# A two-layer encoder trunk on one core: rows times gamma moved to VectorE, the first high part on VectorE, an earlier copy of the sums, and down blocks 32 to 55 in twelve places

## The chip, the cores and the metric

The kernel runs on one core of a Trainium2 chip. The metric is the device time of one execution in microseconds, lower is better. Engines: TensorE (PE) multiplies, VectorE (DVE), ScalarE (ACT) and GpSimd (POOL) work elementwise, SyncE (SP) only issues DMAs. DMAs are issued here by three engines' queues: SP's (q1 in the profile), ACT's (q10) and POOL's gathers (q0).

## The reference

Two layers over 256 tokens of width 1024. The first mixes tokens by dilated attention and pooling, the second by a gated unit; each is followed by a product-key retrieval (`peer`), in which every token takes 128 of 16384 experts:

```python
q = (ht @ w_q).reshape(T, PEER_HEADS, 2, PEER_HALF_DIM)          # ht = rms_norm(x) * gamma
scores = jnp.einsum('thic,hikc->thik', q, sub_keys)
sv, si = lax.top_k(scores, PEER_TOPK)                            # 16 of 128 in each half
cand = sv[:, :, 0, :, None] + sv[:, :, 1, None, :]
best, ci = lax.top_k(cand.reshape(T, PEER_HEADS, 256), PEER_TOPK)
gate = jax.nn.softmax(best, axis=-1)
hid = gelu(einsum('cd,ckd->ck', xb, w_down[eb]))
out = einsum('ck,ckd->cd', gb * hid, w_up[eb])
```

A final RMS norm ends the program. All inputs and the output are float32.

## The kernel before

**Mixing and queries.** Products with the mixer's and the query weights are made as three products of split numbers: a weight block of 128 x 1024 lands in `raw` (four places), `high_part` (ACT, L705) rounds it into `w_hi`, and `low_part` (POOL, L614) subtracts the two into `w_lo` (two places). The activations are split in the same way into `hT_hi` (ACT, L720) and `hT_lo` (DVE, L1453). A layer has 40 such blocks, the last 16 of them for the queries. A next `raw` load waits for `w_lo` of the block that it overwrites (`load`, L468), and a next `w_lo` waits until PE is done with the block two before (L613). The last block of each group of eight waits for its low part before its first product (L1262).

**Normed rows.** Between the query blocks DVE (`norm_tokens`, L1421) works out 1/rms, writes two small scale matrices (L1424), and the first 128 tokens' normed rows `hn` (L1428). POOL waits for them ahead of its low part of query block 5 and multiplies them by gamma, in place in `gff` (L640 to L643). PE multiplies the scale matrices ahead of query block 5 (L1241), DVE copies the result (L1431) and makes `hT` from it (L1437), on which the down phase works. ACT, SP and DVE wait for the product in `gff` by the semaphore `hng_done`.

**Down and up.** 160 tokens ("dense") are multiplied by all 16384 experts' down rows, in 128 blocks of 512 KB, eight matmuls each (`down`, L1292), and later by the up rows (128 blocks, loaded in pairs of 1 MB). For the other 96 tokens only the chosen experts' rows are gathered by POOL (L635), one 512 KB indirect DMA for 128 rows: 96 gathers with down rows and 96 with up rows in a layer. Gather q of the first 53 is issued no sooner than PE has done `pace(q)` = q * 71 // 53 down blocks (L625), no more than five are in flight (L621), and there are ten places (`RING`). DVE takes the dot products of the gathered rows (L1605) between the pieces of its search for the best experts (L1584 to L1699). Results of down blocks (`take_hidden`, L877) fill the arena from its start, over what lay there.

**Where the down blocks lie.** Blocks 0 to 31 use sixteen places: four of `raw`, four of `w_raw`, and eight in the arena (`extra`). From block 32 only the first eight places are used. So SP issues block 16 + j when block j is done, for j = 0 to 23 (L548 to L556; ahead of j = 8 it issues two 1 MB pairs of up rows). It then waits for the first softmax gates (`idg_done`, L557) and moves them with four small DMAs (L559). From block 40 on the load of block b is issued when block b - 8 is done. Of these, blocks 40 to 79 alternate: even ones are issued by SP (`load_down_even`, L539), odd ones by ACT (`load_between`, L944, at L949). From block 80 SP issues all.

**The end of a layer.** ACT takes four banks of the up sums (`UP_BANKS`, L1027) in turn; ahead of the third it copies half of the sparse tokens' sums to other partitions (L1024), which DVE adds to `xs` (L1778) before it adds the dense results (L1814). In the last layer the final norm follows (L693, L1407 to L1417, L1820).

Of the kernel before, what the change touches and what calls it, by code (L numbers as in the profile page):

```python
# [11 lines left out]
ALU = mybir.AluOpType  # L12
# [4 lines left out]
LAYERS = 2  # L17
SEQ = 256
TILES = SEQ // P
DM = 1024  # L20
# [24 lines left out]
BLOCKS = KEYS  # L45
# [20 lines left out]
WIDE_TO = 2 * WIDE  # L66
ROWS = PICKS + MORE
# [14 lines left out]
MORE_AT, MORE_TAKE_AT, MORE_GATES_AT = 26, 34, 40  # L82
# [5 lines left out]
ONES_FROM, ROWS_AT, ONES = 30, 8, 432  # L88
# [99 lines left out]
assert EXTRA_AT + EXTRA_SOON * DM <= QT_AT and ONES_FROM + RAW - 2 >= WIDE_TO - 1  # L188
assert all(WIDE + DOWN_RAW + k <= (EXTRA_AT + k * DM) // DENSE for k in range(EXTRA))
RING_AT = BLOCKS * DENSE  # L190
# [23 lines left out]
def build_trunk(nc, x_d, consts_d, gfin_d, tab_d, iota_d, lncount_d, poolm_d, poolw_d,  # L214
                pscale_d, wm_d, ws_d, bs_d, cnorm_d, subk_d, wd_d, wu_d, gff_d, rows_d, up_rows_d, out_d):
    ctx = ExitStack()
    with ctx:
# [207 lines left out]

        narrow_from = WIDE_TO // WIDE
        down_fills, mix_fills = narrow_from + (BLOCKS - WIDE_TO) // DOWN_RAW, MIX_BLOCKS // RAW
# [4 lines left out]

        def down_slot(b):

            j = b % WIDE
            if b < WIDE_TO and j >= DOWN_RAW:
                return extra[j - DOWN_RAW]
            return down_raw[b % DOWN_RAW]

        def down_arrival(b, l):  # L440

            j = b % WIDE
            if b < WIDE_TO and j >= DOWN_RAW:
                return extra_full[j - DOWN_RAW], (l * narrow_from + b // WIDE + 1) * 16
            j, filled = b % DOWN_RAW, b // WIDE if b < WIDE_TO else narrow_from + (b - WIDE_TO) // DOWN_RAW
# [18 lines left out]
        def _(sp):  # L464
            for l in range(LAYERS):
# [63 lines left out]
                sp.wait_ge(hng_done, l + 1)  # L529
# [18 lines left out]
                for j in range(WIDE + DOWN_RAW):  # L548
                    if j == DOWN_RAW:
                        for p in range(UP_EARLY):  # L550
                            load_up(p, p)
                    sp.wait_ge(w_used, l * LAYER + MIX_BLOCKS + j + 1)
                    if DOWN_RAW <= j < WIDE:
                        load_extra(WIDE + j, j - DOWN_RAW)
                    else:
                        load_down(WIDE + j, j % DOWN_RAW)  # L556
# [38 lines left out]
            for t, k in ((0, 0), (1, 0), (1, 1)):  # L595
# [3 lines left out]
                else:  # L599
                    sp.wait_ge(hn_done, TILES * LAYERS + k + 1)  # L600
# [4 lines left out]
        def _(pool):  # L605
            for l in range(LAYERS):
# [1298 lines left out]
```

## Time and profile before

| | us |
|---|---|
| median of 3 runs | 1501.04 (1500.75 to 1506.45) |
| profiled execution, its own time | 1499.63 |
| its span (first to last instruction) | 1497.8 |
| PE busy | 1470.0 (98%) |
| DVE, POOL, ACT busy | 913.3, 735.3, 488.9 |
| mean granted TensorE clock | 0.996 |
| HBM read | 519 MB, 347 GB/s over the span |

The profile is of one execution; its own time lies 1.4 us below the median. Instruction rows give the start, how long, the engine and line, what is written and read, and in brackets the engine's idle time before with what ended it. Times are from the span's start. Rows with a count merge neighbours of one kind.

### The profile page before, as it was taken

How to read it: one execution, taken by the hardware profiler on the slowest of the kernel's cores; microseconds unless marked ns; L12 is line 12 of the kernel's file. 1: busy time of each engine (PE TensorE's matmuls, PEld its weight loads, DVE VectorE, ACT ScalarE, POOL GpSimd, SP SyncE). 2: the span in 40 equal slices, each digit the busy share in tenths (PEclk: the TensorE clock that was granted, in tenths of full speed). 3: DMA queues.
4: the chain of work that ended last, by engine and by line, in shares of the span. 5: the costliest groups of instructions: out<-in, count | busy, mean ns of one | idle time of the engine just before them, and what ended most of it. 6: DMA issues, size and time to landing. Idle time of an engine off the chain costs nothing.

```text
span 1497.8 us, 28995 instructions
## 1 busy us (share of the span) xinstructions
PE 1470.0 (98%) x10604; PEld 1436.4 (96%) x10604; DVE 913.3 (61%) x2981; ACT 488.9 (33%) x1206; POOL 735.3 (49%) x632
## 2 busy tenths in 40 slices
PE   8999999999999999999999999999999999999996
PEld 6889999999999999999988999999999999999996
DVE  1744999748875444354633499995587834444654
ACT  5663323258870000000065532221888400000001
POOL 6577232348885233343467843323688733333540
PEclk9999999999999999999999999999999999999998
DMA  6456999999999999999945679999899999999994
GB/s 224 160 189 216 359 408 407 406 356 341 361 356 412 415 417 416 417 415 417 376 152 199 212 238 408 407 407 399 319 346 361 372 417 416 416 416 417 415 397 182
DMA packets 126273, 522.86 MB, mean 349 GB/s; under 512 B 14800, under 2 KB 15056, under 8 KB 109392
## 3 DMA queue, kind: packets, MB, share of 16 engines
q1 hardware_dynamic: 56752, 240.01, 42.7%
q0 software_dynamic: 55296, 201.35, 33.9%
q10 hardware_dynamic: 14112, 80.04, 13.1%
q8 instruction: 65, 1.06, 0.3%
q14 instruction: 48, 0.39, 0.1%
HBM read 519.22 MB, written 1.05 MB: 347 GB/s over the span
## 4 chain that ended last, share of the span: by engine, by line
PE 85%; DMA 6%; issue 2%; ACT 2%; DVE 2%; POOL 2%; SPq 0%; DVEq 0%; POOLq 0%; ACTq 0%
PE ps L1042 85%; DMA arena<-in_rows,ret 2%; DMA raw<-in_wd 2%; POOL w_lo L614 2%; DMA spare<-in_wu 1%; PE ps L1050 1%; ACT arena L693 0%; SPq L559 0%; ACT w_hi L705 0%; ACT hT_hi L720 0%; DMA xs<-in_x 0%; DVE xs L1814 0%; DMA raw<-in_wm 0%; DVE arena L1605 0%; DVE xs L1778 0%
## 5 line engine op out<-in xcount | busy, mean ns | idle before, releaser
L1042 PE MATMUL ps<-arena,raw 128*128 128x160 f32 (+1 forms) x2688 | 379.2, 300 | 3.0 <-DMA raw<-in_wd 3.0
L1042 PE MATMUL ps<-arena,w_raw 128*128 128x160 f32 (+1 forms) x2688 | 377.4, 299 | 1.1 <-DVE arena L1732 1.1
L635 POOL DMA_INDIRECT arena<-in_up_rows,ret x192 | 206.5, 1076 | 347.3 <-DVE oh_buf L1745 181.7
L1042 PEld LDWEIGHTS ps<-arena,raw 128*128 128x128 f32 x2688 | 369.8, 191 | 3.5 <-DMA raw<-in_wd 3.5
L1042 PEld LDWEIGHTS ps<-arena,w_raw 128*128 128x128 f32 x2688 | 368.2, 190 | 1.5 <-issue 1.5
L635 POOL DMA_INDIRECT arena<-in_rows,ret x192 | 200.9, 1046 | 257.9 <-DMA arena<-in_rows,ret 72.3
L1745 DVE SCALAR_TENSOR_TENSOR oh_buf<-arena,ret,oh_buf 128x1024 f32<-128x1024 f32 x126 | 163.0, 1294 | 171.7 <-DMA arena<-in_up_rows,ret 165.1
L614 POOL TENSOR_TENSOR w_lo<-raw,w_hi 128x1024 fp32r<-128x1024 f32 x80 | 193.9, 2433 | 93.4 <-PE ps L1042 67.3
L1042 PE MATMUL ps<-arena 128*128 128x160 f32 (+5 forms) x1336 | 184.6, 302 | 0.5 <-DMA spare<-in_wu 0.4
L1042 PEld LDWEIGHTS ps<-arena 128*128 128x128 f32 (+2 forms) x1336 | 178.0, 189 | 3.2 <-issue 1.8
L1605 DVE SCALAR_TENSOR_TENSOR arena<-arena,ps 128x1024 f32<-128x1024 f32 x128 | 153.8, 1216 | 4.0 <-DMA arena<-in_rows,ret 4.0
L1745 DVE SCALAR_TENSOR_TENSOR ret<-arena,ret 128x1024 f32<-128x1024 f32 x62 | 79.7, 1285 | 113.5 <-DMA arena<-in_up_rows,ret 109.9
L651 POOL TENSOR_SCALAR oh_buf<-iota,ret 128x128 f32<-128x128 f32 x160 | 126.6, 795 | 26.8 <-issue 12.4
L999 ACT ACTIVATE arena<-ret 32x1024 f32<-32x1024 f32 x6 | 6.3, 1054 | 395.7 <-PE ps L1042 139.1
L877 ACT ACTIVATE arena<-ps 128x160 f32<-128x160 f32 x152 | 46.0, 302 | 243.6 <-PE ps L1042 223.6
L705 ACT ACTIVATE w_hi<-raw 128x1024 fp32r<-128x1024 f32 x80 | 83.5, 1060 | 80.8 <-DMA raw<-in_wm 53.6
L933 ACT ACTIVATE ret<-iota,ret 128x128 f32<-128x128 f32 x320 | 100.8, 386 | 2.6 <-PE ps L1042 2.6
L1671 DVE SCALAR_TENSOR_TENSOR arena<-iota,ret,ps 128x54 f32<-128x54 f32 x512 | 100.3, 269 | 0.0
L1726 DVE TENSOR_TENSOR arena<-arena,ps 128x512 f32<-128x512 f32 x80 | 55.0, 688 | 67.4 <-PE ps L1042 34.5
L1605 DVE SCALAR_TENSOR_TENSOR arena<-arena,spare 128x1024 f32<-128x1024 f32 x64 | 77.5, 1223 | 19.7 <-DMA arena<-in_rows,ret 19.6
L1042 PE MATMUL ps<-oh_buf,ret 128*128 128x128 f32 x640 | 84.4, 275 | 1.1 <-ACT ret L941 1.1
L1042 PE MATMUL ps<-arena,spare 128*128 (+1 forms) x576 | 82.2, 299 | 0.0
(149 smaller groups left out, 1799.8 us busy)
## 6 DMA issues: line engine op xcount, KB each, us to landing
raw<-in_wd SPq DMA_DIRECT2D x92, 512.0 KB
w_raw<-in_wd SPq DMA_DIRECT2D x92, 512.0 KB
raw<-in_wm SPq DMA_DIRECT2D x80, 512.0 KB
low_rows<-in_wu SPq DMA_DIRECT2D x18, 1024.0 KB
arena<-in_wu SPq DMA_DIRECT2D x18, 1024.0 KB
arena<-in_wd SPq DMA_DIRECT2D x32, 512.0 KB, 13.9
raw<-in_wu SPq DMA_DIRECT2D x14, 1024.0 KB
raw<-in_wu ACTq DMA_DIRECT2D x14, 1024.0 KB
```

Source lines behind the costliest of these rows:

```text
L614: nc.gpsimd.tensor_tensor(w_lo[:, s % WLO, :], raw[:, s, :], whs[:, s].bitcast(F32), ALU.subtract).then_inc(wlo_pool, 1)
L635: nc.gpsimd.indirect_dma_start(ring[s], None, table, bass.IndirectOffsetOnAxis(ap=index, axis=0)).then_inc(row_full[s], 16)
L651: nc.gpsimd.tensor_scalar(oh1g[:, g % 2, k, :], iota[:, :], i1T[:, t:t + 1], gT[:, t:t + 1], ALU.is_equal, ALU.mult).then_inc(oh1_pool, 1)
L705: nc.scalar.activation(whs[:, s], raw[:, s, :], ACT.Copy).then_inc(whi_done, 1)
L877: nc.scalar.activation(block_of(b), down_psum(b % SLOTS), ACT.Gelu_apprx_tanh).then_inc(h_done, 1)
L933: nc.scalar.activation(oh2[:, g % 2, k, :], iota[:, :], ACT.Abs, scale=-1.0, bias=i2T[:, t:t + 1]).then_inc(oh2_far, 1)
L1042: return nc.tensor.matmul(out, lhsT, rhs, start=start, stop=stop, skip_group_check=shared)
L1050: last = nc.tensor.transpose(ps[:, bank + banks[i], o:o + P], src[:, t, c * P:(c + 1) * P], ident[:, :])
L1605: nc.vector.scalar_tensor_tensor(row, row, 1.0, more_rows if more else h_rows, ALU.mult, ALU.mult, accum_out=(more_hid if more else row_hi ...
L1671: step(nc.vector.scalar_tensor_tensor(found[:, (j * 8 + k) % 24, :], places, cif[:, t, n:n + 1], pay[:, h, :], ALU.is_equal, ALU.mult, acc ...
L1726: nc.vector.tensor_tensor(part, part, gates, ALU.mult).then_inc(gmul_done, 1)
L1745: ins = nc.vector.scalar_tensor_tensor(out, row, coef[:, j:j + 1], out, ALU.mult, ALU.add)
```

## The change

Four things are done.

1. DVE multiplies xs by 1/rms and by gamma in one instruction a half, straight into `gff`; POOL's product and `hn` go.
2. The high part of block 0 of layer 0 is made by DVE, as its second instruction, and ACT waits for it in place of making it.
3. In the last layer the copy of the sums stands ahead of bank 1 and not of bank 2.
4. Down blocks 32 to 55 use twelve places (the eight and the last four of the arena's). SP issues all of blocks 16 to 55; the gates' four DMAs come behind block 55's; even and odd blocks alternate between SP and ACT only from 56 on. `write_ones`, which fills the part of the arena behind those places, comes 24 blocks later.

```diff
+MIDDLE, MIDDLE_EXTRA = DOWN_RAW + EXTRA // 2, EXTRA // 2
+MIDDLE_TO = WIDE_TO + 2 * MIDDLE
-MORE_AT, MORE_TAKE_AT, MORE_GATES_AT = 26, 34, 40
+MORE_AT, MORE_TAKE_AT, MORE_GATES_AT = 26, 34, MIDDLE_TO
-ONES_FROM, ROWS_AT, ONES = 30, 8, 432
+ONES_FROM, ROWS_AT, ONES = 54, 8, 432
...
+        def down_place(b):
+
+            if b < WIDE_TO:
+                return b % WIDE, b // WIDE
+            if b < MIDDLE_TO:
+                j, filled = (b - WIDE_TO) % MIDDLE, WIDE_TO // WIDE + (b - WIDE_TO) // MIDDLE
+                return j if j < DOWN_RAW else j + EXTRA - MIDDLE_EXTRA, filled
+            return b % DOWN_RAW, narrow_from + (b - MIDDLE_TO) // DOWN_RAW
...
-                for j in range(WIDE + DOWN_RAW):
-                    if j == DOWN_RAW:
+                for b in range(WIDE, MIDDLE_TO):
+                    if b == WIDE + DOWN_RAW:
                         for p in range(UP_EARLY):
                             load_up(p, p)
-                    sp.wait_ge(w_used, l * LAYER + MIX_BLOCKS + j + 1)
-                    if DOWN_RAW <= j < WIDE:
-                        load_extra(WIDE + j, j - DOWN_RAW)
+                    j, filled = down_place(b)
+                    last = max(n for n in range(b) if down_place(n)[0] == j)
+                    sp.wait_ge(w_used, l * LAYER + MIX_BLOCKS + last + 1)
+                    if j >= DOWN_RAW:
+                        load_extra(b, j - DOWN_RAW)
                     else:
-                        load_down(WIDE + j, j % DOWN_RAW)
+                        load_down(b, j)
                 sp.wait_ge(idg_done, TILES * l + 1)
...
                 for b in range(MIX_BLOCKS):
-                    if b == Q_FROM + 5:
-                        pool.wait_ge(gff_loaded, 16 * (l + 1))
-                        pool.wait_ge(hn_done, TILES * (l + 1))
-                        nc.gpsimd.tensor_tensor(gff, gff, hn[:, 0, :], ALU.mult).then_inc(hng_done, 1)
                     low_part(b, b % RAW, first=l == 0 and b < WLO)
...
                         if l == 0 and first == 0:
-                            high_part(0, 0, first=True)
+                            act.wait_ge(whi_done, 1)
...
                 for g, chunks in enumerate(UP_BANKS):
-                    if g == 2:
+                    if g == (2 if l + 1 < LAYERS else 1):
                         act.wait_ge(row_used, (l + 1) * GATHERS)
...
+                dve.wait_ge(gff_loaded, 16 * (l + 1))
                 for k in range(2):
                     ks = slice(k * HALF, (k + 1) * HALF)
-                    nc.vector.tensor_scalar(hn[:, 0, ks], xs[:, 0, ks], rinv[:, 2, 0:1], None,
-                                            ALU.mult).then_inc(hn_done, 1)
+                    nc.vector.scalar_tensor_tensor(gff[:, ks], xs[:, 0, ks], rinv[:, 2, 0:1], gff[:, ks], ALU.mult,
+                                                   ALU.mult).then_inc(hng_done, 1)
...
             nc.vector.memset(primed[:, :], 0.0).then_inc(primed_set, 1)
+            dve.wait_ge(raw_full[0], 16)
+            nc.vector.tensor_copy(whs[:, 0], raw[:, 0, :]).then_inc(whi_done, 1)
             dve.wait_ge(consts_loaded, 16)
```

The waits for `hng_done` count to 2 * (l + 1) now, and `down_slot` and `down_arrival` take place and fill from `down_place`.

## Rows read from the trace of the kernel before

**Rows 1.** PE's waits, the longest of layer work: us in total, times, longest.
```profile
PE ps L1042 <- DMA raw<-in_wd: 3.0, 2, 2.7
PE ps L1042 <- POOL w_lo L614: 2.5, 6, 0.7
```
**Rows 2.** Timeline, start of the kernel, ACT and PE.
```profile
7.62 1.05 ACT L705 ACTIVATE w_hi<-raw 128x1024 fp32r<-128x1024 f32 x1
8.81 2.04 PE L1042 MATMUL ps<-w_hi,hT_hi 128*128 128x512 f32 x4 [1.18 <-ACT w_hi L705]
...
19.81 1.08 PE L1042 MATMUL ps<-w_lo,hT_hi 128*128 128x512 f32 x4
```
**Rows 3.** Timeline of layer 1's query phase, DVE and POOL.
```profile
836.87 2.41 DVE L1413 SCALAR_TENSOR_TENSOR rtmp<-rinv 128x2 f32<-128x2 f32 x1
842.34 0.87 DVE L1428 TENSOR_SCALAR arena<-xs,rinv 128x512 f32<-128x512 f32 x2
...
843.35 2.39 POOL L643 TENSOR_TENSOR arena<-arena 128x1024 f32<-128x1024 f32 x1 [1.22 <-DVE arena L1428]
845.70 9.46 POOL L614 TENSOR_TENSOR w_lo<-raw,w_hi 128x1024 fp32r<-128x1024 f32 x4
```
**Rows 4.** The same stretch on PE.
```profile
848.16 1.22 PE L1042 MATMUL ps<-hT_hi,w_lo 128*128 128x256 f32 x8 [0.24 <-POOL w_lo L614]
...
851.13 1.12 PE L1042 MATMUL ps<-hT_hi,w_lo 128*128 128x256 f32 x8
852.96 0.36 PE L1042 MATMUL ps<-hT_hi,w_hi 128*128 128x256 f32 x1 [0.70 <-POOL w_lo L614]
```
**Rows 5.** Timeline of the down phases on PE, four blocks a row.
```profile
234.07 8.86 PE L1042 MATMUL ps<-arena,w_raw 128*128 128x160 f32 x64
243.23 7.06 PE L1042 MATMUL ps<-arena,raw 128*128 128x160 f32 x50 [0.31 <-DMA raw<-in_wd]
...
975.99 7.24 PE L1042 MATMUL ps<-arena,raw 128*128 128x160 f32 x39 [2.70 <-DMA raw<-in_wd]
```
**Rows 6.** Windows: PE, PEld, DVE, ACT, POOL busy (x), PEclk, DMA share, GB/s.
```profile
179.00:228.00 49.00, 49.00 (x363) 49.00 (x362) 46.83 (x270) 10.81 (x33) 15.85 (x17) 1.00 1.03 410
976.00:980.00 4.00, 4.00 (x19) 4.00 (x20) 4.00 (x23) 0.41 (x2) 0.00 (x0) 0.64 1.04 410
```
**Rows 7.** DMA queues from 929 to 958: packets, MB, share of 16 engines.
```profile
q0 software_dynamic: 1622, 5.92, 51.3%
q1 hardware_dynamic: 1617, 5.89, 50.9%
```
**Rows 8.** The same from 970 to 1007.9, two of the three queues.
```profile
q1 hardware_dynamic: 1361, 4.91, 32.6%
q10 hardware_dynamic: 1157, 4.20, 27.9%
```
**Rows 9.** All DMA and the gathers' queue, 155.7 to 277.4, layer 0.
```profile
DMA packets 13074, 47.97 MB, mean 394 GB/s; under 512 B 1652, under 2 KB 1652, under 8 KB 12805
...
q0 software_dynamic: 5375, 19.59, 40.5%
```
**Rows 10.** The same from 886.2 to 1007.9, layer 1.
```profile
DMA packets 12977, 47.62 MB, mean 391 GB/s; under 512 B 1642, under 2 KB 1642, under 8 KB 12705
...
q0 software_dynamic: 5455, 19.88, 41.2%
```
**Rows 11.** Gathers with down rows issued from 155 to 277.4 (layer 0).
```profile
L635 POOL DMA_INDIRECT arena<-in_rows,ret x39: 932/932/1796, 164.1 to 274.7; - x39
```
**Rows 12.** DMA issues from 175 to 209: KB each, median us to landing.
```profile
arena<-in_wd SPq DMA_DIRECT2D x8, 512.0 KB, 22.9
```
**Rows 13.** Timeline of SP's queue in layer 1: the gates, then blocks 40 and 42.
```profile
941.90 5.68 SPq L559 DMA_DIRECT2D stats<-ret  x4
958.26 4.68 SPq L514 DMA_DIRECT2D raw<-in_wd  x2
```
**Rows 14.** Timeline of the kernel's end, DVE.
```profile
1486.31 1.28 DVE L1814 TENSOR_TENSOR xs<-xs,ps 128x512 f32<-128x512 f32 x2 [0.56 <-PE ps L1372]
```

More of the change, by code:

```diff
@@ L187 @@
 EXTRA_AT, EXTRA_SOON = 4608, 4
-assert EXTRA_AT + EXTRA_SOON * DM <= QT_AT and ONES_FROM + RAW - 2 >= WIDE_TO - 1
+assert EXTRA_AT + EXTRA_SOON * DM <= QT_AT and ONES_FROM + RAW - 2 >= MIDDLE_TO - 1
 assert all(WIDE + DOWN_RAW + k <= (EXTRA_AT + k * DM) // DENSE for k in range(EXTRA))
+assert all(MIDDLE_TO - EXTRA + k <= (EXTRA_AT + k * DM) // DENSE for k in range(MIDDLE_EXTRA, EXTRA))
+assert MIDDLE_TO % DOWN_RAW == 0
 RING_AT = BLOCKS * DENSE
@@ L424, in blocks @@
                     body(i * slots + j, j)
-        narrow_from = WIDE_TO // WIDE
-        down_fills, mix_fills = narrow_from + (BLOCKS - WIDE_TO) // DOWN_RAW, MIX_BLOCKS // RAW
+        narrow_from = WIDE_TO // WIDE + (MIDDLE_TO - WIDE_TO) // MIDDLE
+        down_fills, mix_fills = narrow_from + (BLOCKS - MIDDLE_TO) // DOWN_RAW, MIX_BLOCKS // RAW
         fills = mix_fills + down_fills
         down_raw = [raw[:, s, :] for s in range(RAW)] + [w_raw[:, s, :] for s in range(WHI)]
+        def down_place(b):
[5 more added lines that the diff above has]
+            return b % DOWN_RAW, narrow_from + (b - MIDDLE_TO) // DOWN_RAW
         def down_slot(b):
[L435 to L438, printed above, removed]
+            j, _ = down_place(b)
+            return extra[j - DOWN_RAW] if j >= DOWN_RAW else down_raw[j]
         def down_arrival(b, l):
[L442 to L445, printed above, removed]
+            j, filled = down_place(b)
+            if j >= DOWN_RAW:
+                per_layer = narrow_from if j - DOWN_RAW >= MIDDLE_EXTRA else WIDE_TO // WIDE
+                return extra_full[j - DOWN_RAW], (l * per_layer + filled + 1) * 16
             if j < RAW:
@@ L527, in _ @@
                     load_extra(DOWN_RAW + k, k)
-                sp.wait_ge(hng_done, l + 1)
+                sp.wait_ge(hng_done, 2 * (l + 1))
                 sp.wait_ge(w_used, l * LAYER + MIX_BLOCKS)
@@ L546, in load_up @@
                                  ).then_inc(up_full[p], 16)
-                for j in range(WIDE + DOWN_RAW):
-                    if j == DOWN_RAW:
+                for b in range(WIDE, MIDDLE_TO):
+                    if b == WIDE + DOWN_RAW:
                         for p in range(UP_EARLY):
                             load_up(p, p)
-                    sp.wait_ge(w_used, l * LAYER + MIX_BLOCKS + j + 1)
-                    if DOWN_RAW <= j < WIDE:
-                        load_extra(WIDE + j, j - DOWN_RAW)
+                    j, filled = down_place(b)
+                    last = max(n for n in range(b) if down_place(n)[0] == j)
+                    sp.wait_ge(w_used, l * LAYER + MIX_BLOCKS + last + 1)
+                    if j >= DOWN_RAW:
+                        load_extra(b, j - DOWN_RAW)
                     else:
-                        load_down(WIDE + j, j % DOWN_RAW)
+                        load_down(b, j)
                 sp.wait_ge(idg_done, TILES * l + 1)
@@ L599, in _ @@
                 else:
-                    sp.wait_ge(hn_done, TILES * LAYERS + k + 1)
+                    sp.wait_ge(hn_done, k + 1)
                 sp.dma_start(out_d[:, t, ks], hn[:, t, ks]).then_inc(out_stored, 16)
@@ L918, in take_rows @@
                 def take_rows():
-                    act.wait_ge(hng_done, l + 1)
+                    act.wait_ge(hng_done, 2 * (l + 1))
                     act.wait_ge(pair_found, PIECES * l + PIECES // 2)
@@ L1433, in norm_tokens @@
                 settle()
-                dve.wait_ge(hng_done, l + 1)
+                dve.wait_ge(hng_done, 2 * (l + 1))
                 for c in range(DC):
@@ L1631, in search @@
                         dve.wait_ge(sc_sb, 8 * (l + 1))
-                        dve.wait_ge(hng_done, l + 1)
+                        dve.wait_ge(hng_done, 2 * (l + 1))
                         step(nc.vector.tensor_copy(numbers, iota[:, :]))
```

## Prediction

> **What bounds the kernel now.** I read the page first, then PE's waits, the timeline around each wait, and last the DMA queues in windows. The page has PE at 98% of the span, so nearly all of the 1497.8 us is matmuls that the change doesn't touch; what can be won is the time in which PE waits or runs at the low clock. The waits name two causes inside the layers: down blocks that land late, 3.0 us in two waits, and POOL's low parts, 2.5 us in six [rows 1]. A third stands at the start, where PE waits 1.18 us for ACT's first high part [rows 2]. So all four edits together have some 8 us within reach, and the one that shifts DMA traffic can lose more than that.
>
> **First high part on DVE.** ACT makes `w_hi` from 7.62 in 1.05 us, between two pairs of `hT_hi`, and PE starts at 8.81 [rows 2]. ACT's row shows no wait for data, so the block had landed by 7.62. DVE is idle then. Its copy of 128x1024 isn't in the trace; the nearest row is its scaling of two halves of 128x512 in 0.87 us [rows 3], the other side is ACT's 1.05. PE also needs the first `hT_hi`, done about 0.1 us after 7.62, so it can start up to 0.95 us sooner, and at worst no sooner. POOL's first low part moves with it. What it is worth depends on the clock: the first four matmuls took 2.04 us and four later ones 1.08 [rows 2], the levels 1.2 and 2.4 GHz. If the clock rises at the same moment as before, 0.9 us at the low level is worth 0.4; if it rises with the work, 0.9. I take **-0.4**, between 0 and -0.95.
>
> **Rows times gamma.** In the query phase POOL multiplies by gamma at 843.35, for 2.39 us, ahead of low part 5, and then makes four low parts back to back from 845.70 [rows 3]. PE catches up twice: eight matmuls from 851.13 take 0.96 us at 0.12 each, and the next starts at 852.96, 0.87 late, of which the row calls 0.70 idle; by the same measure the wait of 0.24 at 848.16 is 0.41 [rows 4]. That is 1.28 us a layer. Without the product low part 5 can start once PE has left block 3. PE wants low part 5 at 847.75; back from there 16 matmuls, some 0.6 us of scale products and one block of 24 matmuls (2.9 us) give 842.3, with the handover 842.6, against 845.70. What is added is DVE's: two halves with two operands in SBUF, for which the nearest is an add of two 128x512 halves in 1.28 us [rows 14], in place of 0.87 [rows 3]. Here lies a hazard that the trace shows: DVE's L1413, 128x2 with two operands in SBUF, took 2.41 us while POOL made a low part, and L1428 only ran behind one [rows 3]. So either POOL waits up to 1.28 us, and ends low part 5 at 846.3 at the latest, 1.4 us ahead of PE's need, or DVE waits up to 2.4 and delays `hT`, which PE wants only at block 8, at 855.8. Low part 7 is wanted at 852.1 and would be ready near 851.1. The waits for `hng_done` on ACT and SP have far more slack: both act in the down phase. I take the whole, 2 x 1.28 = **-2.5**; if the cover of 1.0 us is gone by a further blocked low part (2.4), it is +1.4 a layer, so between -2.6 and +2.8.
>
> **The copy of the sums.** Of the last four dense adds the second pair waits 0.56 us for PE's own last transposes [rows 14], and the rest of the end follows from it. An earlier copy lets only the first pair start earlier. **0**, between -0.3 and 0.
>
> **Twelve places.** One block is 0.524 MB, 1.28 us at the 410 GB/s that all queues move together [rows 6]. PE takes a block every 2.17 us (49 us for 363 records, 16 a block [rows 6]). While only SP and the gathers have work, they send equal numbers of packets [rows 7], so SP lands a block every 2.56 us, slower than PE eats. Loads were landing 22.9 us after their issue, ten blocks later [rows 12]: SP's queue is backed up, and a block in it lands no sooner for having been given a place sooner. What ends that state in the kernel before is ACT's queue, which takes every second block from 41 on: then the two move 9.11 MB in 37.9 us [rows 8], a block in 2.18 us, just PE's pace. The change puts all of blocks 40 to 55 back on SP's queue and lets ACT join 16 blocks later. Against that stand four more places, and the gates' DMAs (5.68 us of issuing at 941.90, then block 40 at 958.26 [rows 13]) no longer ahead of block 40 but ahead of block 56. Block 56 is still issued only when block 48 is done.
>
> I make a budget up to the moment when PE would begin block 56 with no stall. Block 40 began at 243.23 and 975.99, 0.47 and 2.87 us late (the rows ahead of them end a block grid of 2.17; the page calls 0.31 and 2.70 of it idle [rows 5]), so block 56 is due at 277.4 and 1007.9. By 277.4 all queues moved 47.97 MB, 19.59 of it gathers [rows 9]; less 0.16 MB of code fetches that is 53.8 blocks' worth for the down queues and 37.4 gathers. After the change the total is the same, but with two queues gathers get half, until their pace stops them: at block 56 it allows 41.8, against 39 issued before [rows 11], and two are in flight, so 39.7 will have landed, 2.3 more. That leaves 51.5. The down side wants the rest of block 7 (0.5), blocks 12 to 15 (4), the rows for the 32 tokens (1), two up pairs (4) and blocks 16 to 56 (41), 50.5; and ACT's queue will by then have taken blocks 57, 59 and half of 61 out of order, 2.5 more. It is short by 1.5. In layer 1 the moved total is 47.62 MB, 19.88 of it gathers [rows 10]: 52.6 and 37.9, after the change 50.8, short by 2.2. A missing block costs 1.28 us if the gathers give way when PE, and with it their pace, stops, and 3.84 if three queues share evenly: 1.9 to 5.8 us in layer 0, 2.8 to 8.4 in layer 1. I take 3.0 and 4.5, nearer to the low ends. Against the old stalls that is (3.0 - 0.47) + (4.5 - 2.87) = +4.2. The old one in layer 1 also brought the low clock: from 976 to 980 PE was granted 0.64 and did 19 records where 30 fit (363 in 49 us), 1.5 us [rows 6]. That stays, and layer 0's new stall of about the old one's length gets it with even odds, +0.7. Together **+4.9**, between -4.8 (no stall and no low clock at all) and +13.
>
> The ones that ACT writes come 24 blocks later, ahead of the phase that reads them, on an engine busy 10.81 of 49 us [rows 6]: nothing.
>
> A rule of the Trainium skill speaks against this sum: DMA: Bandwidth & Descriptors, Rules for kernel authors, says that spreading DMAs over the issuing engines for bandwidth doesn't help and saves issue time only. By it SP alone would bring what SP and ACT brought, and the sum for this edit would be -4.8. The trace here disagrees: the second queue got 1157 packets of its own beside 1361 [rows 8], and the two together took 60.5% of the engines' time where SP alone had 50.9% [rows 7]. The same page's section Queues, rings and completion order, that each DMA engine goes round its queues packet by packet, fits rows 7 and 8.
>
> **Sum.** -0.4 - 2.5 + 0 + 4.9 = +2.0 us against the profiled execution's 1499.63; the median lies 1.4 above it, so 1501.04 + 2.0 = **1503**. 0.5%, about 7.5 us, is what a measurement can tell from no change.
>
> **Rivals.**
> - *The stall is gone.* SP keeps up through block 55, for instance because the gathers stay behind their pace or the backlog has drained by then; the four places give 8.7 us of lead. For it: the longest wait stands at block 40, right at the change from sixteen places to eight. Against it: the equal shares of rows 7. -0.4 - 2.5 - 4.8 = -7.7, **1493.3**. Chance 0.26.
> - *The stall moves to block 56 at its old size.* The budget is short, but by less than I have it. -0.4 - 2.5 = -2.9, **1498**. Chance 0.17.
> - *The low parts are blocked in turn.* DVE's two halves and POOL's low parts lock each other out so that nothing is won there: 1503 + 2.5 = **1505.5**. For it: the 2.41 us of rows 3; against: the 1.0 us of cover. Chance 0.08.
> - *Slower: SP's queue starves at its join with ACT's.* From ACT's first load at block 49 SP has a third, blocks 50 to 56 come every 3.8 us, and PE stops in pieces, with the low clock in both layers: the upper ends, 5.8 and 8.4 us, give +10.9, with two low clocks +12.4, less 2.9, +9.5, **1510.5**. It decides from 7.5 us more than before, that is 10.4 us of added stalls. For it: 22.9 us from issue to landing, and the backlog only grows until block 49. Against it: the gathers stop at their pace. Chance 0.14.
>
> The forecast has the remaining 0.35. Faster by over 0.5% is the first rival, 0.26; slower by over 0.5% the last, 0.14; within it the rest, 0.60. The range is 1492 to 1509.5: it takes in the first rival with all of the start's gain and most of the last.
>
> **What would show it.** Right: PE's waits for `raw<-in_wd` gone at block 40 and back at or just before block 56 in both layers, near 277 and 1005, longer in layer 1; SP and gathers with equal packets up to about 265 and 995; the low clock behind the stalls. POOL's six waits down to four or fewer, low parts in the query phase never back to back for more than two. PE's first product at 7.9 to 8.6. The last four adds unmoved against PE's last transposes. Wrong: no wait for down blocks in either layer, or a total wait above 10 us; SP's queue landing blocks 40 to 55 at 2.2 us each or faster; a wait for `hT` at query block 8.

## The result and the profile after

The changed kernel took 1513.55 us, the median of six runs (1510.56 to 1514.69), where the kernel before took 1500.89 beside it (six runs, 1498.09 to 1506.45). The ratio is 1.0083, with a 95% interval of 1.0063 to 1.0103. It is slower by some 12.6 us; 1503.0 was forecast, in a range that ended at 1509.5. The profiled execution took 1510.56 us, with a span of 1508.8; it is the fastest of the six, so what follows is the changed kernel at its best. One execution of a kernel below (e3, 1689.88 us at a mean granted clock of 0.85) was in a slow state and is left out of every number.

PE's waits in the changed kernel (us in total, times, longest), where before had [rows 1]:

```profile
PE ps L1051 <- DMA raw<-in_wd: 6.8, 3, 3.4
...
PE ps L1051 <- DMA arena<-in_wd: 6.0, 6, 1.5
PE ps L1051 <- DMA w_raw<-in_wd: 2.2, 2, 1.1
...
PE ps L1051 <- POOL w_lo L627: 0.3, 1, 0.3
```

Down blocks account for 15.0 us in eleven waits instead of 3.0 in two; the low parts went from 2.5 us in six waits to 0.3 in one. So VectorE's part did its work and the blocks' loads lost much more than it won. PE's timeline in layer 0 shows where; block 40 starts at 240.05, block 44 at 249.11, block 56 at 286.70 (compare [rows 5]):

```profile
240.05 8.86 PE L1051 MATMUL ps<-arena 128*128 128x160 f32 x64
249.11 10.12 PE L1051 MATMUL ps<-arena,raw 128*128 128x160 f32 x64 [0.21 <-DMA raw<-in_wd]
259.36 5.00 PE L1051 MATMUL ps<-arena,w_raw 128*128 128x160 f32 x32
265.43 4.98 PE L1051 MATMUL ps<-arena,w_raw 128*128 128x160 f32 x32 [1.07 <-DMA w_raw<-in_wd]
271.66 2.44 PE L1051 MATMUL ps<-arena 128*128 128x160 f32 x16 [1.25 <-DMA arena<-in_wd]
274.40 2.44 PE L1051 MATMUL ps<-arena 128*128 128x160 f32 x16 [0.29 <-DMA arena<-in_wd]
278.31 5.01 PE L1051 MATMUL ps<-arena 128*128 128x160 f32 x32 [1.47 <-DMA arena<-in_wd]
286.70 3.53 PE L1051 MATMUL ps<-arena,raw 128*128 128x160 f32 x24 [3.38 <-DMA raw<-in_wd]
```

Block 40's wait is gone. From block 44 on each block starts 2.56 instead of 2.17 us after the one before: the row from 249.11 holds four blocks in 10.12 us where the row above it holds four in 8.86, although PE is hardly called idle in it, since it waits between the records of one row. From block 50 on the pieces are larger. Against blocks that follow one another in 2.17 us from block 0 on, block 56 starts 11.9 us late in layer 0 and 11.0 in layer 1. In the kernel before it was 0.6 and 4.7 us late: the stalls of 0.47 and 2.87 at block 40, and the low clock behind the second. (The 15.0 us of the page are less than 11.9 + 11.0, since it leaves out most of the small waits.) No low clock follows here: outside the start and the last 8 us the granted clock is 1.00. In the five other executions the mean granted clock was 0.993 to 0.995 against 0.997 here, which for this span is an estimated 6 to 13 us more at the low level; so some of them most likely had it, and that would be the 3 us that the median lies above this profile. No trace of them was kept.

The same by stages, from PE's first matmul of one stage to that of the next, in us. "Down phase" in the table and in the experiments is the stretch from the first down matmul to the first matmul of the gates, which stands behind block 76 (77 blocks of the 128):

| stage | before | after | difference |
|---|---|---|---|
| first to second transposes of `xs` (start) | 11.39 | 9.35 | -2.04 |
| query phase, layer 0 and 1 | 57.25, 57.27 | 55.89, 55.89 | -1.36, -1.38 |
| down phase, layer 0 | 169.66 | 179.77 | +10.11 |
| down phase, layer 1 | 172.43 | 178.93 | +6.50 |
| last gate matmul to up phase, layer 0 and 1 | 27.31, 26.63 | 26.51, 26.50 | -0.80, -0.13 |
| last matmul to the end of the span | 11.8 | 11.88 | +0.1 |

Of the 169.66 us before, 1.37 come from a wait for ScalarE (`ret`, L941; 1.1 by the page) just ahead of the gates and not for a block. `xs` also landed 0.7 us later in this execution. Together, with differences of at most 0.4 us in the stages not shown, that is the spans' 11.0 us.

DMA queues of the changed kernel while SP's loads and the gathers are alone, from 205 to 262 (packets, MB, share of 16 engines), to be set beside [rows 7]:

```profile
q1 hardware_dynamic: 3195, 11.61, 51.2%
q0 software_dynamic: 3191, 11.61, 51.0%
```

They are again in step: 11.61 MB in 57 us is a block (0.524 MB) in 2.57 us. Then, from 262 to 286, with ScalarE's queue from 264.40 on:

```profile
q1 hardware_dynamic: 1380, 4.33, 46.1%
q0 software_dynamic: 912, 3.29, 34.7%
q10 hardware_dynamic: 513, 1.89, 20.2%
```

SP's queue in the same stretch (start, duration, engine, line, operation, count). The four loads of blocks 52 to 55 (L515) are followed by the gates (L572), and block 56 (first of L525 at 261.97) comes behind them, some 13 us before PE is due at it (274.8):

```profile
242.41 8.70 SPq L515 DMA_DIRECT2D arena<-in_wd  x4
251.16 6.84 SPq L572 DMA_DIRECT2D stats<-ret  x4
261.97 6.42 SPq L525 DMA_DIRECT2D raw<-in_wd  x2
```

### The profile page after: what moved, and what is told of

Its sections match the earlier page's. It is cut to its first block, busy times and chain, and to the rows that moved or that the text cites. A ratio compares the mean times of both kernels' runs of the same rounds, so it can differ in the third digit from the quotient of the medians.

```text
span 1508.8 us, 28936 instructions
## 1 busy us (share of the span) xinstructions
PE 1472.1 (98%) x10604; PEld 1434.5 (95%) x10604; DVE 921.3 (61%) x2982; ACT 488.0 (32%) x1205; POOL 725.2 (48%) x630
## 3 DMA queue, kind: packets, MB, share of 16 engines
HBM read 519.22 MB, written 1.05 MB: 345 GB/s over the span
## 4 chain that ended last, share of the span: by engine, by line
PE 88%; DMA 8%; ACT 1%; issue 1%; POOL 1%; DVE 1%; DVEq 0%; SPq 0%; ACTq 0%; POOLq 0%
PE ps L1051 87%; DMA w_raw<-in_wd 3%; DMA raw<-in_wd 3%; POOL w_lo L627 1%; PE ps L1059 1%; DMA spare<-in_wu 1%; DMA xs<-in_x 0%; ACT arena L702 0%; DMA raw<-in_wm 0%; ACT w_hi L714 0%; ACT arena L773 0%; DVE xs L1826 0%; ACT L692 0%; DVE arena L1574 0%; ACT hT_hi L729 0%
## 5 line engine op out<-in xcount | busy, mean ns | idle before, releaser
L1051 PE MATMUL ps<-arena,raw 128*128 128x160 f32 (+1 forms) x2560 | 361.4, 299 | 7.4 <-DMA raw<-in_wd 6.8
L1051 PE MATMUL ps<-arena,w_raw 128*128 128x160 f32 (+1 forms) x2560 | 361.5, 299 | 3.0 <-DMA w_raw<-in_wd 2.2
L1051 PEld LDWEIGHTS ps<-arena,raw 128*128 128x128 f32 x2560 | 350.7, 190 | 9.5 <-DMA raw<-in_wd 9.5
L1051 PEld LDWEIGHTS ps<-arena,w_raw 128*128 128x128 f32 x2560 | 350.8, 190 | 5.4 <-DMA w_raw<-in_wd 4.8
L648 POOL DMA_INDIRECT arena<-in_rows,ret x192 | 194.7, 1014 | 257.3 <-PE ps L1051 89.0
L1051 PE MATMUL ps<-arena 128*128 128x160 f32 (+5 forms) x1592 | 221.7, 302 | 6.6 <-DMA arena<-in_wd 6.0
L1051 PEld LDWEIGHTS ps<-arena 128*128 128x128 f32 (+2 forms) x1592 | 213.2, 189 | 11.0 <-DMA arena<-in_wd 8.2
L1051 PE MATMUL ps<-arena,low_rows 128*128 (+1 forms) x576 | 81.2, 299 | 0.0
```

The costliest lines, as they stand in the source:

```text
L648: nc.gpsimd.indirect_dma_start(ring[s], None, table, bass.IndirectOffsetOnAxis(ap=index, axis=0)).then_inc(row_full[s], 16)
L1051: return nc.tensor.matmul(out, lhsT, rhs, start=start, stop=stop, skip_group_check=shared)
```

## The experiments

All times below are medians, with the ratio to the kernel before in the same comparison (1499.3 to 1500.4 us, 1500.9 beside the changed kernel) and its 95% interval. Where two experiments of different comparisons are set against each other by their medians, that shift of up to 1.6 us is in the difference. Diffs are against the changed kernel unless the text says otherwise.

**e1: the old places, the rest of the change kept.** `MORE_GATES_AT`, `ONES_FROM`, `down_place` and SP's loop as in the kernel before.

> The changed kernel with down blocks 32 to 55 put back as they were (eight places, ScalarE issuing every second block from 40 on, the gates behind block 39); the gamma product on VectorE, the first high part on VectorE and the sooner copy of the sums are kept. Theory (the whole loss is in the blocks' loads): the down phases take 169.7 and 172.4 us again, the query phases keep their 1.4 us each and the start keeps 0.4 to 1.35 us, so 1500.9 - 2.7 - (0.4 to 1.35) = 1497 us, 1496 to 1498. Rival (the VectorE parts also push on the down phase, by the other order of the picks and gates behind them): down phases above 172 us and a time of 1500 or more.

Measured: 1495.72 us, ratio 0.9971 (0.9954 to 0.9988). The loss is gone, and the three small parts show as a gain. The down phases of the profiled execution took 174.94 and 171.90 us. The first is worse than the 169.7 expected, though the code is that of before: PE waited 3.76 us for block 40, and the low clock followed, as layer 1 of before had it. PE's timeline, and the windows before, in and behind the low clock (PEclk is the number ahead of the last two):

```profile
243.37 8.90 PE L1038 MATMUL ps<-arena,raw 128*128 128x160 f32 x43 [3.76 <-DMA raw<-in_wd]
```

```profile
233.00:239.00 6.00, 5.93 (x44) 5.69 (x43) 5.93 (x22) 2.17 (x6) 1.27 (x3) 1.00 1.03 402
242.50:249.00 6.50, 5.63 (x21) 5.63 (x22) 6.46 (x42) 0.75 (x2) 0.19 (x1) 0.50 1.03 408
```

21 records in 5.63 busy us, where the window before has 44 in 5.93: 1.2 instead of 2.4 GHz, from 242.26 for 6.83 us. So the wait at block 40 differs from execution to execution, and the profile of before had caught a short one in layer 0 (0.47 us).

**e2: the kernel before with the first high part on VectorE alone.** Diff against the kernel before:

```diff
-                            high_part(0, 0, first=True)
+                            act.wait_ge(whi_done, 1)
...
+            dve.wait_ge(raw_full[0], 16)
+            nc.vector.tensor_copy(whs[:, 0], raw[:, 0, :]).then_inc(whi_done, 1)
```

> The kernel before with one part of the change: the first high part on VectorE. Prediction's theory: ScalarE's 1.05 us copy is replaced by a shorter one and only 0.4 us comes off the first product, 1500.5 us. Rival (from the two profiles: start to second transposes 11.39 against 9.35 us, though x landed 0.7 us later): TensorE's clock rises sooner and 1.3 to 2 us come off, 1499 to 1499.6 us.

Measured: 1498.90 us, ratio 0.9996 (0.9979 to 1.0013). It can't be told from no change, nor the two theories from one another; e12 repeats it where the down phases are steady.

**e3: the kernel before with the twelve places alone.** The rest of the diff, without e2's lines, the gamma product and the sooner copy.

> The kernel before with the twelve places for down blocks 32 to 55 alone. Theory (all of the loss is here): the down phases grow by 10.1 and 6.5 us, 1500.9 + 16.6 = 1517.5 us, 1516 to 1519. Rival (the VectorE parts bring the collision by moving the searches or gathers): 1505 or less, since the blocks' loads alone would fit.

Measured: 1516.45 us, ratio 1.0119 (1.0094 to 1.0144). All of the loss is in this edit: some 17 us, and the rest of the change takes 3 to 5 back. The loss needs none of the VectorE parts.

**e4: twelve places, but two queues.** ScalarE issues the odd blocks from 41, as soon as their place is free.

```diff
+ALT_FROM = 40
...
                 for b in range(WIDE, MIDDLE_TO):
+                    if b >= ALT_FROM and b % 2:
+                        continue
...
+                    n = b + MIDDLE
+                    if ALT_FROM <= n < MIDDLE_TO and n % 2:
+                        nc.scalar.dma_start(down_slot(n), wd_d[l, n]).then_inc(down_arrival(n, l)[0], 16)
                     n = b + DOWN_RAW
```

> The changed kernel, twelve places kept, but the odd blocks from 41 to 55 issued by ScalarE as soon as their place is free (12 blocks ahead), as it does from 57 on in the changed kernel. Theory (a queue's share: with SP's and the gathers' queue alone each gets 51% of the engines' time, and a block lands every 2.56 us against the 2.17 us of its product): with two queues for blocks they get more, the waits between block 44 and 56 go, and the down phases come to 167 to 169 us each: 1513.5 - (10.8 to 12.8) - (10 to 12) = 1490 to 1494 us. Rival 1 (the places, their order or the 13 us gap between block 55's and block 56's issue make the loss, not the queue): 1508 to 1513.5. Rival 2 (the Trainium skill, DMA: Bandwidth & Descriptors, Rules for kernel authors: to spread loads over issuing engines brings no bandwidth): 1513.5, no change.

Measured: 1494.69 us, ratio 0.9968 (0.9953 to 0.9984), e1's time, and 17 to 19 us below the changed kernel (by the ratios, by the medians). It is the queue that costs and not the places. Every wait from block 41 on is gone; there are new ones ahead of it, at blocks 37 to 40, since ScalarE's blocks take from the engines while SP's older ones are still in its queue:

```profile
234.62 2.44 PE L1057 MATMUL ps<-arena,w_raw 128*128 128x160 f32 x16 [1.26 <-DMA w_raw<-in_wd]
238.14 2.44 PE L1057 MATMUL ps<-arena,w_raw 128*128 128x160 f32 x16 [1.08 <-DMA w_raw<-in_wd]
241.02 2.44 PE L1057 MATMUL ps<-arena,w_raw 128*128 128x160 f32 x16 [0.44 <-DMA w_raw<-in_wd]
245.15 5.02 PE L1057 MATMUL ps<-arena 128*128 128x160 f32 x35 [1.69 <-DMA arena<-in_wd]
```

The queues from 225 to 245 in e4 show the second queue adding to the blocks' share: 37.4% + 27.0%, against the 51.2% that one queue had in the changed kernel.

```profile
q0 software_dynamic: 829, 3.01, 37.8%
q1 hardware_dynamic: 824, 2.99, 37.4%
q10 hardware_dynamic: 603, 2.14, 27.0%
```

**e5: the changed kernel with two up pairs loaded later.** Two loads of 1.05 MB for the up phase stand in SP's queue ahead of block 24, over 200 us before they are read.

```diff
                 for b in range(WIDE, MIDDLE_TO):
-                    if b == WIDE + DOWN_RAW:
-                        for p in range(UP_EARLY):
-                            load_up(p, p)
...
                 blocks(sp, load_down_even, MORE_GATES_AT, ALONE_FROM, DOWN_RAW)
+                for p in range(UP_EARLY):
+                    load_up(p, p)
                 blocks(sp, load_down_again, ALONE_FROM, BLOCKS, DOWN_RAW)
```

> The changed kernel with one thing moved: the loads of the first two up pairs (1.05 MB each, four blocks' worth), which SP issues behind down block 23, are issued behind block 79. Theory (SP's queue is short of bytes, at 2.56 us a block beside the gathers'): it is 4 x 2.56 = 10.2 us further on from block 24 on, so the waits of blocks 44 to 55 (6.8 and 6.5 us) go in both layers; block 56, whose issue waits for block 48 and stands behind the gates, keeps 0 to 3.5 us. 1513.5 - 13.3 = 1500 us, down to 1493. Rival 1 (the up pairs' bytes cost nothing, since they only fill gaps; the share of the queue or the order of places makes the loss): 1510 or more. Rival 2 (the gathers take up what is freed, as they are on an own queue): 1506 to 1510.

Measured: 1498.84 us, ratio 0.9987 (0.9973 to 1.0002), 14.7 us below the changed kernel. In the profiled execution the waits of blocks 44 to 55 are gone, and block 56 starts 0.87 us late in layer 0 and keeps this wait in layer 1, with 3.41 us of low clock behind it:

```profile
994.74 6.55 PE L1050 MATMUL ps<-arena 128*128 128x160 f32 x47
1003.78 8.46 PE L1050 MATMUL ps<-arena,raw 128*128 128x160 f32 x48 [2.49 <-DMA raw<-in_wd]
```

This execution took 1492.16 us, the fastest of twelve and 6.7 below the median. So most executions lost more in the down phases than it shows, and e6, which differs in the places and queues alone, is 11.3 us faster by the medians: beside SP's one queue the later up pairs mend a good part and not all.

**e6: old places and the two up pairs later.** e1 with e5's edit.

> The changed kernel without its twelve places (as e1) and with the same two up pairs behind block 79. Theory: e1's waits at block 40 (3.9 us in layer 0, 2.3 in layer 1) and the low clock that follows each (6.83 and 3.41 us at half speed, so 3.4 and 1.7 us lost) go together: 1495.7 - 11.3 = 1484.5 us, 1483 to 1488. Rival (the stall at block 40 comes from its late issue, eight blocks ahead behind block 31 that ends 17.4 us before, and not from the queue's backlog): no change, 1494 to 1496.

Measured: 1487.53 us, ratio 0.9901 (0.9880 to 0.9922). It beats both kernels, the one before by 12.8 us by the medians. PE's longest waits:

```profile
PE ps L1045 <- DMA xs<-in_x: 6.0, 1, 6.0
PE ps L1045 <- DVE arena L1560: 0.5, 1, 0.5
PE ps L1037 <- POOL w_lo L613: 0.3, 1, 0.3
```

No down block is waited for. Both down phases take 167.79 us, to the hundredth, which is what they cost with every block there. Against that floor the kernel before lost 1.9 (1.37 of it the wait for ScalarE) and 4.6 us in its profiled execution, e1 7.2 and 4.1, the changed kernel 12.0 and 11.1.

**e7: blocks 56 to 63 issued as soon as their places are free.** The twelve places free block 56's after block 44; the change still waits for 48. The edit lets SP (even) and ScalarE (odd) issue them twelve blocks ahead, 56 and 58 ahead of the gates.

```diff
+                def load_down_soon(b, j):
+                    sp.wait_ge(w_used, l * LAYER + MIX_BLOCKS + b - MIDDLE + 1)
+                    load_down(b, j)
...
+                for b in range(MIDDLE_TO, SOON_TO - DOWN_RAW + 4, 2):
+                    load_down_soon(b, b % DOWN_RAW)
                 sp.wait_ge(idg_done, TILES * l + 1)
...
+                for b in range(SOON_TO - DOWN_RAW + 4, SOON_TO, 2):
+                    load_down_soon(b, b % DOWN_RAW)
+                blocks(sp, load_down_even, SOON_TO, ALONE_FROM, DOWN_RAW)
...
+                    n = b + MIDDLE
+                    if MIDDLE_TO <= n < SOON_TO and n % 2:
+                        nc.scalar.dma_start(down_slot(n), wd_d[l, n]).then_inc(down_arrival(n, l)[0], 16)
```

> The changed kernel, but blocks 56 to 63 are issued when their place is free (12 blocks ahead, which the twelve places give them), the even ones by SP (56 and 58 ahead of the gates), the odd ones by ScalarE. Theory A (the 3.5 and 3.3 us wait of block 56 is the late issue): it goes, 1513.5 - 6.8 = 1506.7 us. Theory B (short of bytes all the same): ScalarE's blocks from 57 on take a share from the blocks 50 to 55 that stand in SP's queue, the waits move ahead and the sum is kept, 1511 to 1514.

Measured: 1510.38 us, ratio 1.0058 (1.0037 to 1.0079): 3.2 us below the changed kernel, between the theories and nearer to B. Block 56's wait falls from 3.38 to 1.02 us, and what it loses comes back ahead of it, first of all at blocks 49 and 50:

```profile
261.43 2.44 PE L1063 MATMUL ps<-arena,w_raw 128*128 128x160 f32 x16 [1.45 <-DMA w_raw<-in_wd]
266.01 2.44 PE L1063 MATMUL ps<-arena,w_raw 128*128 128x160 f32 x16 [2.14 <-DMA w_raw<-in_wd]
...
285.08 5.16 PE L1063 MATMUL ps<-arena,raw 128*128 128x160 f32 x36 [1.02 <-DMA raw<-in_wd]
```

**e8: old places, but blocks 40 to 55 on SP's queue alone.** Diff against e1:

```diff
+ALT_FROM = 56
...
-                blocks(sp, load_down_even, MORE_GATES_AT, ALONE_FROM, DOWN_RAW)
+                blocks(sp, load_down_again, MORE_GATES_AT, ALT_FROM, DOWN_RAW)
+                blocks(sp, load_down_even, ALT_FROM, ALONE_FROM, DOWN_RAW)
...
-                    if MORE_GATES_AT <= n < ALONE_FROM and n % 2:
+                    if ALT_FROM <= n < ALONE_FROM and n % 2:
```

> The changed kernel with down blocks in the old eight places (as e1), but 40 to 55 issued by SP alone, as in the changed kernel. Theory (what counts is the one queue beside the gathers'): SP's queue lands a block every 2.56 us, and the loss against e1 is that of the changed kernel or more, since the gates stand ahead of block 40 and the loads are issued later: 1508 to 1517 us. Rival (the twelve places and their order make the loss): e1's time, 1495 to 1498.

Measured: 1507.96 us, ratio 1.0048 (1.0030 to 1.0067). Taking ScalarE's queue away costs e1 12.2 us by itself, at the low end of what was expected. The twelve places on top (with the gates behind block 55 in place of 39) made it 5.6 us worse by the medians (1513.55), not better; in the two profiled executions the down phases are as good as equal (178.89 and 179.28 here, 179.77 and 178.93 in the changed kernel).

PE's row at block 49 and ScalarE's first load show that pieces come with SP's and the gathers' queue alone:

```profile
263.99 6.79 PE L1040 MATMUL ps<-arena,raw 128*128 128x160 f32 x48 [1.01 <-DMA raw<-in_wd]
...
266.47 0.33 ACTq L947 DMA_DIRECT2D raw<-in_wd  x1
```

**e9: the kernel before with the two up pairs later, nothing else.** e5's edit on the kernel before.

> The kernel before with the first two up pairs' loads behind block 79 and nothing else of the change. Theory (in the kernel before, too, the down phases lose 2 to 8 us to block 40's wait and the low clock behind it, and this goes; the VectorE parts' own worth is what then stands between this kernel and e6): 1487.5 + 2 x 1.37 (query phases) + 1.7 (start) = 1492 us, 1490.5 to 1493. Rival (the VectorE parts give nothing of their own): 1487 to 1488.5.

Measured: 1491.29 us, ratio 0.9935 (0.9911 to 0.9958). Both down phases take 167.79 us here too. The three small parts of the change are what stands between this and e6: 3.8 us by the medians.

**e10: the changed kernel with two gathers under way instead of five.**

```diff
-RING, IN_FLIGHT, RING_FIRST = 10, 5, 2
+RING, IN_FLIGHT, RING_FIRST = 10, 2, 2
```

> The changed kernel with at most two instead of five gathers under way, for the row gathers of the whole kernel. Theory (the gathers' queue never ran empty, so they kept their 51% of the engines; with two in flight it runs empty between them and a gather comes every 2.9 to 3.3 us instead of 2.56): the blocks of SP get the rest, the waits of blocks 44 to 56 shrink by half or more in both layers, 1500 to 1508 us, unless the gathers' own lateness takes it back at their dots. Rival (how often a gather is issued doesn't matter, SP's queue is held by its own 25 us latency): 1512 to 1515.

Measured: 1608.32 us, ratio 1.0721 (1.0681 to 1.0762), a plain miss in size. The half of the theory on the blocks held. The queues from 190 to 210:

```profile
q1 hardware_dynamic: 1611, 5.88, 73.7%
q0 software_dynamic: 618, 2.27, 28.6%
```

SP's queue took what the gathers left, and no wait for a down block is among PE's longest. But the gathers fell behind, VectorE with them, and PE then waited for what VectorE makes:

```profile
PE ps L1331 <- DVE ret L1701: 34.7, 2, 20.0
PE ps L1051 <- issue: 33.3, 9, 12.5
```

The down phases took 212.14 and 208.89 us. So the gathers have no slack of that size to give; the loads that were not yet due had it (e5).

**e11: twelve places, two queues, and the up pairs later.** e4 with e5's edit.

> The changed kernel with twelve places, blocks 41 to 55 (odd) issued by ScalarE 12 ahead as in e4, and the first two up pairs behind block 79. Theory (the twelve places harm nothing once the bytes are there): no wait in the down phases, the time of e6, 1486.5 to 1488.5 us. Rival (the longer lead of ScalarE's blocks takes share from SP's 36 to 40, as in e4): one or two waits of about 1 us a layer are left, 1489 to 1492.

Measured: 1487.26 us, ratio 0.9907 (0.9880 to 0.9934). It is e6's time, with both down phases at 167.79 us. Twelve places do no harm when the bytes are there, and bring nothing. With twelve places the four cases are then: one queue 1513.55, one queue and the up pairs later 1498.84, two queues 1494.69, both 1487.26.

**e12: e9 with the first high part on VectorE.** e2's diff on e9.

> e9 (the kernel before with two up pairs behind block 79, whose down phases have no wait) with the first high part on VectorE added. Theory (the first product starts 0.3 to 0.9 us sooner and TensorE's clock rises sooner after it, so the start to the second transposes takes 9.6 instead of 11.15 us): 1491.3 - 1.5 = 1489.8 us. Rival (the prediction's size, 0.4 us, the clock's rise not hanging on it): 1490.9 us, with a start of 10.8 us.

Measured: 1490.55 us, ratio 0.9932 (0.9913 to 0.9952); 0.7 us below e9 by the medians, between the theories and nearer to the prediction's 0.4. PE at the start, first e9, then e12:

```profile
8.82 2.04 PE L1041 MATMUL ps<-w_hi,hT_hi 128*128 128x512 f32 x4 [1.18 <-ACT w_hi L704]
10.66 1.91 PE L1041 MATMUL ps<-w_hi,hT_lo 128*128 128x512 f32 x4
12.37 1.90 PE L1041 MATMUL ps<-w_lo,hT_hi 128*128 128x512 f32 x4
14.07 1.12 PE L1041 MATMUL ps<-w_hi,hT_hi 128*128 128x512 f32 x4
```

```profile
7.94 2.04 PE L1041 MATMUL ps<-w_hi,hT_hi 128*128 128x512 f32 x4 [0.38 <-DVE w_hi L1466]
9.78 1.36 PE L1041 MATMUL ps<-w_hi,hT_lo 128*128 128x512 f32 x4
10.97 1.09 PE L1041 MATMUL ps<-w_lo,hT_hi 128*128 128x512 f32 x4
```

The first product comes 0.88 us sooner (7.94 against 8.82) and the clock is up about 3.8 us sooner (10.35 against 14.12), so this stage is 2.1 us shorter in these two executions (9.02 against 11.15). In the eleven profiled executions with the VectorE copy, the changed kernel's among them, the stage took 8.73 to 9.75 us, in the three without it 10.80 to 11.39. The two groups' means, 9.20 and 11.11, lie 1.9 us apart. Where the rest of that goes in the medians stays open: the profiled e12 was 0.85 and 0.6 us longer in two later stages and e9 1.6 us in another, and one profile a kernel can't settle half a microsecond.

## Why the prediction was wrong

**The step that failed is the price of a missing block.** It read: "A missing block costs 1.28 us if the gathers give way when PE, and with it their pace, stops, and 3.84 if three queues share evenly: 1.9 to 5.8 us in layer 0, 2.8 to 8.4 in layer 1. I take 3.0 and 4.5, nearer to the low ends." The stalls measured 11.9 and 11.0 us, above even the upper ends. The nearest case was the slower rival, SP's queue starving at its join with ScalarE's, which had 0.14: PE stops in pieces over blocks 50 to 56, 9.6 of the 11.9 us in layer 0. Its 1510.5 was still 3 us short, its low clocks don't stand in the profile, and the join is not what starts the pieces, as the third point below shows. The prediction's own sign of being wrong, a total wait above 10 us, came (15.0), and its place for the stall, "at or just before block 56", was twelve blocks late.

Three things stood behind the price:

- *The gathers gave way late, and in part.* From 153.1 to 274.8, when block 56 would have been due, they moved 20.43 MB, 39.0 gathers, against 39.7 forecast, and both down queues together 51.2 blocks' worth against 51.5. The budget of bytes was right; ScalarE's queue had even moved only 0.70 MB of it out of order, 1.3 blocks and not 2.5, so by the bytes 0.6 of a block was missing and not 1.5. But the gathers kept step with SP packet for packet to 262 (51.0% against 51.2%), while PE had been losing time since block 44; only then did they fall to 34.7%, with POOL's issues of them waiting up to 5.5 us for PE. The price up to 262 was 2.56 us a block, not 1.28. e10 shows the same from the other side: made to give way, both down phases are over 40 us above e6's.
- *The shortage was taken at one moment.* The budget asked only whether block 56 is there when due. Yet a queue that brings a block in 2.56 us against 2.17 is late by 0.39 at each block once its lead is used up, and that was block 44: 2.3 us by the start of block 49, before ScalarE's first load was issued (264.40).
- *Mean bytes aren't a landed block.* A block comes in 16 parts, and PE waits for the last. By the trace's landing times the parts of block 36 were spread over 4.6 us (223.51 to 228.13) and those of block 48 over 5.1 us. Block 52 had its first part at 263.46 and its last at 271.62, block 54 its first at 267.31 and last at 278.26, block 55 270.30 and 280.83, block 56 273.88 and 286.66. PE went on at 271.66, 278.31, 280.88 and 286.70, each time within 0.05 us of the last part. So while the first part of block 55 landed (270.30), the last of block 52 had not. In e6 the spread stays between 1.8 and 4.1 us in the same stretch. Mostly it is one part that lags: of block 56 all others had landed by 279.40 and the last came 7.3 us later, of block 55 those on record by 276.71 and the last 4.1 us later. This starts before ScalarE's queue moves anything (its first packet is at 267.90): block 50's parts already took from 259.30 to 265.38, and PE began the block at 265.43. In e8 the parts of block 49 took from 254.62 to 263.94, 9.3 us, all ahead of ScalarE's first load at 266.47. So a third queue isn't needed for it; what holds the one part back stays open.

**What drained the queue** was in the budget, four units for two up pairs, and was read as a fixed cost. e5, e6, e9 and e11 show that it was the largest thing still to be had in the kernel before: 2.1 MB that nobody reads for over 200 us, ahead of blocks that PE is waiting for. Moved, it is worth 14.7 us in the changed kernel and 9 in the one before.

**The start of the comparison was off as well.** The stall of 0.47 us in layer 0 was taken as the kernel's; e1 and e2, with the same loads, had 3.76 and 1.45 + 3.05 us of waits there and a low clock for 6.83 us each. A wait at the edge of a full queue varies, and one profile shows one draw of it. The low clock, kept in layer 1 and given even odds in layer 0, came in neither layer of the changed kernel's profile, though its longest stop was 3.38 us, against 3.76 in e1; ahead of it stood short stops instead of full speed, but whether that decides it is not shown. That a stop brings the low clock was seen after 2.17 us in layer 1 of e1 and not after 3.38 here, so the length of the stop alone doesn't decide it.

**The queue share: right**, and with it the objection to the Trainium skill. SP and the gathers were in step at 51% each, and SP landed blocks every 2.56 us. The Trainium skill's page DMA: Bandwidth & Descriptors, Rules for kernel authors, says that spreading DMAs over issuing engines brings no bandwidth; e8 against e1 (+12.2 us for one queue instead of two) and e4 against the changed kernel (-18.9 us) disagree where a third queue competes. The total stays at 410 GB/s; the split is what changes. By the rule the edit would have made no loss.

**Rows times gamma: right.** -1.36 and -1.38 us against -1.25 a layer. POOL's low parts and the products on DVE in layer 1, to be set beside [rows 3]:

```profile
846.02 2.41 POOL L627 TENSOR_TENSOR w_lo<-raw,w_hi 128x1024 fp32r<-128x1024 f32 x1 [0.48 <-PE ps L1051]
848.90 5.54 POOL L627 TENSOR_TENSOR w_lo<-raw,w_hi 128x1024 fp32r<-128x1024 f32 x2 [0.47 <-PE ps L1051]
```

```profile
843.16 2.40 DVE L1422 SCALAR_TENSOR_TENSOR rtmp<-rinv 128x2 f32<-128x2 f32 x1
...
845.98 2.72 DVE L1433 TENSOR_SCALAR arena<-consts,rinv 128x128 f32<-128x128 f32 x2
848.63 3.55 DVE L1438 SCALAR_TENSOR_TENSOR arena<-xs,rinv,arena 128x512 f32<-128x512 f32 x2
```

POOL now waits for PE and not PE for POOL. The hazard that was named came, and on both sides: DVE's two halves took 3.55 us instead of some 1.3, and two low parts 5.54 instead of 4.8. It fitted in the cover.

**First high part: right way, the size open.** The copy took 0.69 us (7.62 to 8.31 on DVE), and the first product moved from 8.81 to 8.46 in the changed kernel, though its `xs` landed 0.7 us later. 0.4 was taken, at most 0.95; the medians of e12 and e9 give 0.7, the stage itself 1.9. The prediction let the clock rise at the same moment or with the work, 0.9 us sooner; it rose 3.8 us sooner (e12 against e9), and that case had no price.

**The copy of the sums: right, nothing.** The second pair of the last adds waits for PE in both kernels and starts 0.31 us after PE's last matmul in both (1486.31 - 1486.00 and 1497.23 - 1496.92). In the changed kernel:

```profile
1495.16 1.28 DVE L1826 TENSOR_TENSOR xs<-xs,ps 128x512 f32<-128x512 f32 x2 [1.84 <-PE ps L1381]
1497.23 1.28 DVE L1826 TENSOR_TENSOR xs<-xs,ps 128x512 f32<-128x512 f32 x2 [0.79 <-PE ps L1381]
```

In sum: the three small parts were put at -2.9 and came to -3.8 (e9 to e6), the twelve places at +4.9 and came to some +17 (e3).

## What to carry to other kernels

When a queue of loads is backed up, more places ahead of it were worth nothing here (e8 against the changed kernel, e6 against e11); count what each queue brings in the time of one product, beside every other queue that is busy, and look first for loads in it that are due much later. A shortage has to be priced block by block from the moment the lead is used up, at the share the queue really gets, and for the last of a load's parts and not for its mean. A stall that sits on such an edge varies between executions, so one profile's size of it is no base for a sum; here the spread of the times themselves (1494 to 1508 us before, 1486 to 1488 once it was gone) fits that.

## What the runs showed of the hardware that was not expected

- A load's 16 parts land over 2 to 5 us while the queue keeps up, and over 6 to 13 us later in a backlog, mostly by one part that lags (block 52: 263.46 to 271.62; block 56: 273.88 to 286.66, all but the last by 279.40). With two busy queues and no third, 9.3 us were seen (e8, block 49).
- With one queue's requests under way limited, its share went to the other: with two gathers instead of five 28.6% against 73.7% (e10, 190 to 210), at 409 GB/s in total.
- A stop of PE in the down phase was followed by 1.2 GHz for 3.41 us (after 2.17 us of waiting, e1 in layer 1) or 6.83 us (after 3.76, e1 in layer 0), and the eleven stops in the changed kernel's profile, up to 3.38 us, by none.
- Starting PE's first product 0.88 us sooner brought the higher clock about 3.8 us sooner (e12 against e9).
